# Differenced value rows in stick-breaking attention, and later table loads in the state-space scan

## What is computed

```python
def stick_breaking_attention(q, k, v):      # A[t,s] = beta_ts * prod_{s<j<t}(1 - beta_tj), s < t
...
        log_beta = jax.nn.log_sigmoid(z)
        log_1m = jnp.where(causal, log_beta - z, 0.0)
        later = lax.cumsum(log_1m, axis=3, reverse=True) - log_1m
        w = jnp.where(causal, jnp.exp(log_beta + later), 0.0)
        outs.append(jnp.einsum('bhqk,bkhd->bqhd', w.astype(v.dtype), v[:, :kv_len]))
```

```python
def s5_mixer(xn, w_in, ...):                # grouped state-space model, chunkwise scan, then a gated projection
    u = (xn @ w_in).astype(f32)
...
        bu = jnp.einsum('tbgh,gph->tbgp', u_t.astype(jnp.complex64), b_bar)
        a_cum, s = lax.associative_scan(binop, (a_elems, bu), axis=0)
        y = jnp.einsum('tbgp,ghp->tbgh', s, c_mat).real
```

## Time and profile before

| what | us |
|---|---|
| median of 3 runs (2297.76 to 2300.46) | 2300.3 |
| the profiled execution, whole | 2300.35 |
| its span, first to last instruction | 2298.6 |
| PE busy | 2239.3 (97%) |
| DVE busy | 1275.2 (55%) |
| ACT busy | 984.8 (43%) |
| POOL busy | 394.9 (17%) |

### The profile page before, as it was taken

One profiled execution on the slowest core, in us unless ns is written; L12 is line 12 of the kernel. 1 busy time (PEld: TensorE's weight loads), 2 busy tenths in 40 slices (PEclk: granted clock), 3 DMA queues, 4 the chain that ended last, 5 costly groups with the idle time before them and its releaser, 6 DMA issues.

```text
span 2298.6 us, 30269 instructions
## 1 busy us (share of the span) xinstructions
PE 2239.3 (97%) x11479; PEld 1806.8 (79%) x11479; DVE 1275.2 (55%) x2273; ACT 984.8 (43%) x1835; POOL 394.9 (17%) x472
## 2 busy tenths in 40 slices
PE   7899999999999999999979999999999999999999
PEld 6777777688877787878868888888888668888887
DVE  6965565755645444454583555464444685554643
ACT  7445555533554545363432423233344654232322
POOL 7742131126202030300000000000034230000000
PEclk9999999999999999999999999999999999999999
DMA  7354212134232222315462232322222102323222
GB/s 224 117 170 128 74 56 92 43 105 161 97 119 62 87 89 77 97 60 192 147 212 86 80 110 80 104 92 93 91 99 88 52 19 74 110 87 97 92 102 81
DMA packets 182444, 232.51 MB, mean 101 GB/s; under 512 B 29499, under 2 KB 110866, under 8 KB 182302
## 3 DMA queue, kind: packets, MB, share of 16 engines
q1 hardware_dynamic: 159406, 205.64, 27.9%
q10 hardware_dynamic: 22896, 24.94, 3.4%
HBM read 213.74 MB, written 21.00 MB: 102 GB/s over the span
## 4 chain that ended last, share of the span: by engine, by line
PE 87%; DVE 6%; issue 2%; ACT 2%; POOL 1%; DMA 1%; SPq 0%; ACTq 0%; POOLq 0%; DVEq 0%
PE G L2199 25%; PE G L2201 25%; PE G L2200 25%; DVE w_lo L1756 1%; PE X L2208 1%; PE X L2319 1%; PE X L2330 1%; PE X L2307 1%; PE X L2333 1%; DMA big<-s_u 1%; PE X L2303 1%; POOL big L1235 1%; PE X L2218 1%; DVE u_lo L1801 1%; PE X L2311 1%
## 5 line engine op out<-in xcount | busy, mean ns | idle before, releaser
L2199 PE MATMUL G<-w_hi,u_hi 128*128 128x512 f32 x1536 | 622.1, 405 | 4.0 <-issue 2.1
L2201 PE MATMUL G<-w_hi,u_lo 128*128 128x512 f32 x1536 | 600.9, 391 | 0.0
L2200 PE MATMUL G<-w_lo,u_hi 128*128 128x512 f32 x1536 | 599.2, 390 | 0.0
L1756 DVE SCALAR_TENSOR_TENSOR w_lo<-raw,par,w_hi 128x512 fp32r<-128x512 f32 x496 | 373.3, 791 | 401.1 <-ACT w_hi L1256 398.1
L1256 ACT ACTIVATE w_hi<-raw,par 128x512 fp32r<-128x512 f32 x496 | 318.2, 714 | 342.1 <-PE G L2201 340.2
L2199 PE MATMUL G<-u_hi,w_hi 128*128 128x512 f32 (+1 forms) x1168 | 458.3, 392 | 0.3 <-DVE w_lo L1756 0.2
L2201 PE MATMUL G<-u_hi,w_lo 128*128 128x512 f32 (+1 forms) x1168 | 446.0, 382 | 0.0
L2200 PE MATMUL G<-u_lo,w_hi 128*128 128x512 f32 (+1 forms) x1168 | 446.0, 382 | 0.0
L2199 PEld LDWEIGHTS G<-w_hi,u_hi 128*128 128x128 f32 x1536 | 289.1, 188 | 71.0 <-issue 9.3
L2201 PEld LDWEIGHTS G<-w_hi,u_lo 128*128 128x128 f32 x1536 | 288.5, 188 | 62.2
L2200 PEld LDWEIGHTS G<-w_lo,u_hi 128*128 128x128 f32 x1536 | 289.3, 188 | 59.4 <-issue 1.9
(11 more groups left out here) (316 smaller groups left out, 2388.8 us busy)
## 6 DMA issues: line engine op xcount, KB each, us to landing
raw<-in_ffn_w_up SPq DMA_DIRECT2D x88, 512.0 KB, 4.7
raw<-in_e_w_in SPq DMA_DIRECT2D x56, 512.0 KB, 4.7
raw<-in_o_w_in SPq DMA_DIRECT2D x56, 512.0 KB, 4.5
raw<-in_ffn_w_down SPq DMA_DIRECT2D x40, 512.0 KB, 4.3
raw<-in_e_w_out SPq DMA_DIRECT2D x16, 512.0 KB, 4.6
raw<-in_o_w_out SPq DMA_DIRECT2D x16, 512.0 KB, 4.3
raw<-in_a_w_glu SPq DMA_DIRECT2D x16, 512.0 KB, 4.5
raw<-in_w_kv SPq DMA_DIRECT2D x16, 512.0 KB, 4.6
```

What stands on the lines that cost most here:

```text
L1756: V.scalar_tensor_tensor(w_lo[:, n % HL, k], raw[:, n % RAW, k], gain(name, k0 + k), w_hi[:, n % HL, k].bitcast(F32), ALU.mult, ALU.subtract)\
L2199: pe.matmul(out, lh, rh, start=start, stop=False)
L2200: pe.matmul(out, lh, rl, start=False, stop=False)
L2201: return pe.matmul(out, ll, rh, start=False, stop=stop)
```

## The change

Stick-breaking: the differences of the products are no longer made, neither on DVE nor on POOL, and the buffers and memsets for them go. PE transposes the products themselves, as soon as two rounds after the scores (three before), and sums three rounds after them (four before), so the stage has one slot less, and three of its rounds instead of four are hosted by the value chunk. ACT's copy out of the transpose becomes 1 - x, an Identity with scale -1 and a bias read from a column of ones. The scan that reuses a buffer now waits for the transpose of its old content, where it waited for the differencing. The values are differenced instead, once: behind the last block of each value chunk ACT issues a copy of its rows, shifted down by one partition, into rows 16 to 19 of big (127 partitions, and one more DMA for the rows that cross a tile), and DVE subtracts it from the values, 128 by 512 at a time, four times for each chunk: for the first chunk in the host's positions 3 to 6, for the second in rounds 8 to 11.

State-space: ACT issues zl(4) and zl(5) in slot 8 and zl(6) and zl(7) in slot 9, all behind a new wait for the load of u(7).

The diff, its core:

```diff
@@ -481,39 +481,37 @@
+            s.values = (values - 1, values)
-            s.slots = s.rounds + 5
+            s.slots = s.rounds + 4
-            plan_chunks([("v", "N", dict(dst=1, step=2))], [(s, -4)])
-            stage("between", host=s, host_at=4, host_end=s.slots)
+            plan_chunks([("v", "N", dict(dst=1, step=2))], [(s, -5)])
+            for a in range(2):
+                for m in range(4):
+                    mark("value_step", s.i, a, m)
+            stage("between", host=s, host_at=3, host_end=s.slots)
...
@@ -678,6 +676,7 @@
+        S5_NEXT = {8: (4, 5), 9: (6, 7)}
@@ -853,10 +852,11 @@
-        def sb_weight(t):
-            i = t // 2 % TT
-            o = 8192 + P * (i * (i + 1) + t % 2 * (i + 1))
-            return bigf[:, o:o + P * (i + 1)]
+        value_shifted = sem("value_shifted")
+        row_before = big[:, 16:20, :]
+
+        def value_rows(a):
+            return att[:, 0:8, :].rearrange("p (t a) n -> p t a n", a=2)[:, :, a, :]
@@ -1219,21 +1219,6 @@
-                if n == sb_down.n:
-                    for t, (hd, i) in enumerate(sb_mix.steps):
...
-                        pool.wait_ge(*at_("sb_product", sb_mix.i, t))
-                        if t >= 2 * TT:
-                            pool.wait_ge(*at_("sb_turned", sb_mix.i, t - 2 * TT))
-                        pool.tensor_tensor(sb_weight(t)[:, 0:L - 1], sb_prod(t)[:, 1:L], sb_prod(t)[:, 0:L - 1],
-                                           ALU.subtract).then_inc(*by(sb_step(t), sb_mix.i, t))
@@ -1387,12 +1372,20 @@
+            def shift_values(chunk, a):
+
+                act.wait_ge(*at_("operand", chunk, "v", 3))
+                if a:
+                    act.wait_ge(*at_("value_step", sb_mix.i, 0, 3))
+                act.dma_start(row_before[1:P, :, :], value_rows(a)[0:P - 1, :, :]).then_inc(value_shifted, 16)
+                act.dma_start(row_before[0:1, 1:4, :], value_rows(a)[P - 1:P, 0:3, :]).then_inc(value_shifted, 16)
@@ -1402,13 +1395,14 @@
-                if 0 <= u - 3 < s.rounds:
-                    n = P * ((u - 3) % TT + 1)
-                    for t in (2 * u - 6, 2 * u - 5):
+                if 0 <= u - 2 < s.rounds:
+                    n = P * ((u - 2) % TT + 1)
+                    for t in (2 * u - 4, 2 * u - 3):
                         if t >= 4:
-                            act.wait_ge(*at_("sb_summed", s.i, u - 5))
+                            act.wait_ge(*at_("sb_summed", s.i, u - 4))
                         act.wait_ge(*at_("sb_turned", s.i, t))
-                        nc.scalar.activation(sb_turned(t)[:, 0:n], G[:, t % SB_TURN, 0:n], ACT.Copy)\
+                        nc.scalar.activation(sb_turned(t)[:, 0:n], G[:, t % SB_TURN, 0:n], ACT.Identity,
+                                             bias=one_c, scale=-1.0)\
                             .then_inc(*by("pt_copied", s.i, t))
@@ -1528,8 +1522,10 @@
-                    if k < 4:
-                        s5_load_zl(k + 4)
+                if t == 8:
+                    act.wait_ge(s5_u_loaded[KT - 1], 16)
+                for k in S5_NEXT.get(t, ()):
+                    s5_load_zl(k)
@@ -1630,6 +1626,8 @@
                                         .then_inc(*by("operand", s.i, "v", m))
+                                    if m == 3 and s.i in sb_mix.values:
+                                        shift_values(s.i, s.dst)
@@ -1974,6 +1972,14 @@
+            def value_step(a, m):
+
+                dve.wait_ge(value_shifted, 32 * (a + 1))
+                if a == 0 and m == 0:
+                    link("dve", dve, V.memset(row_before[0:1, 0, :], 0.0))
+                v = value_rows(a)[:, m, :]
+                V.tensor_tensor(v, v, row_before[:, m, :], ALU.subtract).then_inc(*by("value_step", sb_mix.i, a, m))
@@ -1987,16 +1993,12 @@
                     if t >= 4:
-                        dve.wait_ge(*at_(sb_step(t), s.i, t - 4))
+                        dve.wait_ge(*at_("sb_turned", s.i, t - 4))
                     V.tensor_tensor_scan(sb_prod(t)[:, 0:L][:, ::-1], sb_keep(t)[:, 0:L][:, ::-1],
                                          bias_tile[:, 384 - P * i:512][:, ::-1], 1.0, ALU.mult, ALU.max)\
                         .then_inc(*by("sb_product", s.i, t))
-                t = 2 * u
-                dve.wait_ge(*at_("sb_product", s.i, t))
-                if t >= 2 * TT:
-                    dve.wait_ge(*at_("sb_turned", s.i, t - 2 * TT))
-                V.tensor_tensor(sb_weight(t)[:, 0:L - 1], sb_prod(t)[:, 1:L], sb_prod(t)[:, 0:L - 1],
-                                ALU.subtract).then_inc(*by(sb_step(t), s.i, t))
+                if 2 * TT <= u < 3 * TT:
+                    value_step(1, u - 2 * TT)
@@ -2048,6 +2050,8 @@
+                        if s.host is sb_mix and 3 <= b < 7:
+                            value_step(0, b - 3)
@@ -2345,28 +2349,28 @@
-                if 0 <= u - 3 < s.rounds:
-                    if u == 3:
-                        pe.wait_ge(*at_("sb_zero", s.i))
-                    for t in (2 * u - 6, 2 * u - 5):
-                        pe.wait_ge(*at_(sb_step(t), s.i, t))
+                if 0 <= u - 2 < s.rounds:
+                    for t in (2 * u - 4, 2 * u - 3):
+                        pe.wait_ge(*at_("sb_product", s.i, t))
                         pe.wait_ge(*(at_("pt_copied", s.i, t - SB_TURN) if t >= SB_TURN else at_(*s.gfreed[t])))
-                        for j in range((u - 3) % TT + 1):
-                            ins = pe.transpose(G[:, t % SB_TURN, j * P:(j + 1) * P], sb_weight(t)[:, j * P:(j + 1) * P],
+                        for j in range((u - 2) % TT + 1):
+                            ins = pe.transpose(G[:, t % SB_TURN, j * P:(j + 1) * P], sb_prod(t)[:, j * P:(j + 1) * P],
                                                ident[:, :])
                         ins.then_inc(*by("sb_turned", s.i, t))
-                if 0 <= u - 4 < s.rounds:
-                    pair, i = (u - 4) // TT, (u - 4) % TT
+                if 0 <= u - 3 < s.rounds:
+                    pair, i = (u - 3) // TT, (u - 3) % TT
...
                     if i == 0:
                         pe.wait_ge(*(at_("sb_y", s.i, pair - 1) if pair else at_(*s.gfreed[SB_SUM])))
+                        if pair % TT == 0:
+                            pe.wait_ge(*at_("value_step", s.i, pair // TT, 3))
```

More of the change, by code:

```diff
@@ L483, in plan_sb @@
             values = len(plan)
+            s.values = (values - 1, values)
             s.steps = [(2 * p + e, i) for p in range(s.heads // 2) for i in range(TT) for e in range(2)]
             s.rounds = len(s.steps) // 2
-            s.slots = s.rounds + 5
+            s.slots = s.rounds + 4
             s.gfreed = [("operand", values, "v", m) for m in range(4)]
-            plan_chunks([("v", "N", dict(dst=1, step=2))], [(s, -4)])
-            stage("between", host=s, host_at=4, host_end=s.slots)
-            for u in range(4, s.slots):
+            plan_chunks([("v", "N", dict(dst=1, step=2))], [(s, -5)])
[3 more added lines that the diff above has]
+            stage("between", host=s, host_at=3, host_end=s.slots)
+            for u in range(3, s.slots):
                 plan_sb_slot(s, u)
@@ L507, in plan_sb_slot @@
                     mark("sb_product", s.i, t)
-                    mark(sb_step(t), s.i, t)
-            if 0 <= u - 3 < s.rounds:
-                for t in (2 * u - 6, 2 * u - 5):
+            if 0 <= u - 2 < s.rounds:
+                for t in (2 * u - 4, 2 * u - 3):
                     mark("sb_turned", s.i, t)
                     mark("pt_copied", s.i, t)
-            if 0 <= u - 4 < s.rounds:
-                mark("sb_summed", s.i, u - 4)
-            if u - 5 >= 0 and (u - 5) % TT == TT - 1:
-                mark("sb_y", s.i, (u - 5) // TT)
+            if 0 <= u - 3 < s.rounds:
+                mark("sb_summed", s.i, u - 3)
+            if u - 4 >= 0 and (u - 4) % TT == TT - 1:
+                mark("sb_y", s.i, (u - 4) // TT)
         def plan_down(kt, first=0, host=None, host_at=0, y=None):
@@ L1388, in act_slot @@
                     act.wait_ge(*at_("aux_ready", s.aux["ot" if s.akind == "A" else "pv", s.heads - 1]))
+            def shift_values(chunk, a):
[4 more added lines that the diff above has]
+                act.dma_start(row_before[0:1, 1:4, :], value_rows(a)[P - 1:P, 0:3, :]).then_inc(value_shifted, 16)
             def act_sb(s, u):
-                if u - 5 >= 0 and (u - 5) % TT == TT - 1:
-                    act.wait_ge(*at_("sb_summed", s.i, u - 5))
-                    nc.scalar.activation(big[:, (u - 5) // TT, :], G[:, SB_SUM, :], ACT.Copy)\
-                        .then_inc(*by("sb_y", s.i, (u - 5) // TT))
+                if u - 4 >= 0 and (u - 4) % TT == TT - 1:
+                    act.wait_ge(*at_("sb_summed", s.i, u - 4))
+                    nc.scalar.activation(big[:, (u - 4) // TT, :], G[:, SB_SUM, :], ACT.Copy)\
+                        .then_inc(*by("sb_y", s.i, (u - 4) // TT))
                 if u < s.rounds:
@@ L2347, in pe_sb @@
```

(14 more changed lines are left out.)

18 lines of the change are left out of this document (1 added, 17 removed).

## The result

| | before | after |
|---|---|---|
| median of the runs, us | 2299.3 (2297.8 to 2300.5, 4 runs) | 2354.0 (2353.5 to 2355.6, 4 runs) |
| ratio after / before | | 1.0235, 95% interval 1.0221 to 1.0248 |
| span of the profiled execution, us | 2298.6 | 2352.4 |
| busy PE, us | 2239 | 2242 |

A forecast was written before the change was run, and what follows sets the result against it. PE carries 87% of the chain, so savings count only where PE waits or runs at the lower clock. 5.3 + 2.7 + 1.5 + 1.7 - 1.25 = 9.95 us off 2300.35 gives 2290.4 us, range 2287.0 to 2295.5.

The forecast's parts named there:

- the start of the stick-breaking stage: Behind the value chunk, PE's 0.69 us wait for ACT becomes about 1.95: +1.25 us, between +0.5 and +2.5.
- The cover that I named: First chunk's row copy, 7 to 9 us, is covered: DVE has nothing to do before the high part preceding ACT's table load.
- issue two copies: At the stick-breaking start, ACT's two copy issues cost 0.33 us and up each, 0.8 in all.
- has until round 8: Stick-breaking: the second chunk's row copy is not needed until round 8.
- State-space, -5.3: u(4) lands earlier, PE's 4.66 us wait before V(4) goes, DVE's chains and B(4) shift: -5.3 us, -5.4 to -3.5.
- Rival 2: State-space: ACT's new wait for u(7) delays zl(4) and Y(4), taking the 5.3 us gain; 2295.7 us, chance 0.08.
- Steady part, -2.7: Stick-breaking rounds: differences go, PE sets the pace, late rounds four apart 8.54 us instead of 9.38: -2.7 us.
- rival 3: Stick-breaking: the shorter distance makes PE wait in every 512 round, so the gain does not come; 2295 us, chance 0.06.
- The end, -1.5 and -1.7: Stick-breaking end: PE's 1.65 us wait shrinks to about 0.15 (-1.5), low clock before the last sums goes (-1.7).
- one fewer: Clock case: the second low-clock stretch, after the stick-breaking stage, may not come; 2288.7 us, chance 0.11.
- rival 1: Clock: new PE waits may bring 1.2 GHz stretches, 2292.1 or 2293.8 us (0.13), or one fewer comes, 2288.7 (0.11).
- Rival 4: Stick-breaking: Identity outside Sigmoid's table gives every round two table loads on ACT, 70 us longer; 2360 us, chance 0.04.

The follow-up runs named there:

- e6_cut_126: The whole change with the copy of 127 rows cut into 126 + 1; 2292.9 us against 2300.1 for the kernel before.
- e1_split: The whole change with the copy of 127 rows cut into 112 + 15; 2292.6 us against 2299.0 for the kernel before, ratio 0.9974.
- e5_sp_issue: The whole change with rows copied in 112 + 15 and the copies issued on SP's queue, not ACT's; 2286.3 us against 2300.1 for the kernel before.
- e4_swapped: The changed kernel with its two copies issued in the other order, the little one first, the 127 rows last; 2352.5 us.
- e2_tables: The kernel before with the state-space part of the change alone, stick-breaking as before; 2292.2 us, ratio 0.9971.
- e9_values_sp: Kernel before plus the stick-breaking part alone, rows in 112 + 15, copies issued on SP's queue; 2291.7 us against 2299.7, ratio 0.9965.

## Why the prediction was wrong

**The failed step.** It is the start of the stick-breaking stage, priced at +1.25 us and at most +2.5; it came to 62.3 us more of waiting and some 3.7 of low clock. The term in it that failed is the copy of the rows: "half as much takes 6.9 us in the full stretch, so 7 to 9 us". I took bytes from a load of 128 rows and gave the copy the same width. It moved its megabyte in 43 us. The cover that I named, up to ACT's table load about 12 us later, was right in kind and 30 us short. The prediction asked nowhere how many engines share the copy. With the height 127 held against the rule that the other heights bear out (e6_cut_126), and by 26 GB/s an engine, which these traces show, the sum would have come out on the side of slower.

**The second failed step**, of the same edit: "issue two copies (0.33 and up each, 0.8 in all)". My bound came from one short issue. Behind a copy on one engine an issue was held 33.5 and 34.1 us. And even at full width, three issues took 3.9 us (e1_split). I had named what stands behind ACT at the start (high part, sigmoids, the copy that PE waits for) and that each would be late by as much; only the amount was wrong. With it, PE's wait at the start is 36.1 us in the kernel after, 4.97 in e1_split and 1.00 in e5_sp_issue, against a forecast of 1.95 and at most 3.2 (0.69 + 2.5). The terms of that forecast, 0.8 for the issues and 0.65 for the sigmoids, also sum to 1.45 and not to its 1.25; with no issue on ACT, e5_sp_issue shows 0.31 over the 0.69 of before. The second copy "has until round 8": enough for data that lands in 6 us, but in e4_swapped DVE waits 26.9 us for it, and in the kernel after it was its issue that PE paid for.

**State-space, -5.3: right.** u(4) lands 6.9 us after its issue instead of 13.4, and the 4.66 us wait is gone. PE's timeline, before (a row ahead of the stretch, for the offset that the execution already had) and after:

```profile
1166.67 1.12 PE L2441 MATMUL X<-att,big 128*64 128x128 f32 x16 [0.95 <-DVE work L1964]
```

```profile
1165.44 1.11 PE L2445 MATMUL X<-att,big 128*64 128x128 f32 x16 [0.94 <-DVE work L1962]
...
1186.84 1.17 PE L2419 MATMUL X<-big,att 128*64 128x64 f32 x32 [2.68 <-DVE work L1962]
1189.87 1.15 PE L2445 MATMUL X<-att,big 128*64 128x128 f32 x16 [0.78 <-DMA att<-s_toeplitz]
1193.61 1.15 PE L2428 MATMUL X<-ident,work 64*64 64x64 f32 x32 [1.56 <-DVE work L1962]
```

B(4) starts at 1193.61 against 1200.35, 6.74 earlier, of which 1.23 were there at the first row: 5.5 us, for 5.35 forecast. V(7) now waits for DVE (2.68), no longer for a load, as the step has it. The new wait's price is visible and small: Y(4) waits 0.78 us for its table, and B(4) still waits for DVE, so nothing of it reaches the end. Rival 2 is false. Over whole runs the part is worth 6.8 us (e2_tables, 4.6 to 8.7).

**Steady part, -2.7: right.** In the kernel after, behind the two copies, PE's first matmuls of rounds four apart (before: the earlier trace rows), and DVE's scans:

```profile
1906.78 0.49 PE L2350 MATMUL X<-big,att 64*128 64x128 f32 x4
...
1915.31 0.49 PE L2350 MATMUL X<-big,att 64*128 64x128 f32 x4
...
1923.85 0.49 PE L2350 MATMUL X<-big,att 64*128 64x128 f32 x4
```

```profile
1921.06 1.81 DVE L1997 TENSOR_TENSOR_SCAN work<-att,bias_tile 128x384 f32<-128x384 f32 x2 [1.26 <-ACT att L1396]
1923.62 1.23 DVE L1997 TENSOR_TENSOR_SCAN work<-att,bias_tile 128x512 f32<-128x512 f32 x1 [0.76 <-ACT att L1396]
```

8.54 us to the last, where it was 9.38; DVE waits for ACT in each round. The 1 - x copies take 534 ns in the median (L1404) against 446 for the plain ones (L1411), 0.09 more each, within the 0 to 0.1 of the forecast. The shorter distance between scores and transpose costs nothing in the steady part: rival 3 is false.

**The end, -1.5 and -1.7: right.** The wait of 1.65 us is 0.19 + 0.17, and no low clock comes before the last sums. The 2.13 us wait stayed. The stretch at half clock behind it stayed in the kernel after (0.66 over 1939 to 1943) and did not come in e5_sp_issue, which has the form of the case "one fewer" of rival 1. Its reason, that the wait before the last sums is gone, does not hold: that wait is gone in the kernel after and in e9_values_sp as well, and there the stretch comes (granted clock 0.79 over 1881 to 1889 in e9_values_sp, 1.00 over 1871 to 1879 in e5_sp_issue, with the same stage of 95.1 us). What decides it stays open, and it is luck of the execution as far as these runs show. Without the start, the stick-breaking terms sum to -5.9; the stage of e5_sp_issue measured -5.9 with a start wait that is 0.3 longer than before.

**Rival 4** (table loads for Identity) is false: there are as many table loads as before, and in e5_sp_issue the stage's table load stands once ahead of its first sigmoid.

So the forecast for the kernel with its copies at full width and off ACT would have been 2290.4 + (1.0 - 1.95) = 2289.5, and 2287.8 for an execution without the second stretch (1.7), for 2286.3 measured. The rest of the gap is of the size of what the state-space part gave over its forecast (6.8 for 5.3). Every other step was read from rows of the same work; the copy was priced by bytes, and the issues by one issue in a quiet place.

## What to carry to other kernels

Price a DMA by its shape and not by its bytes: ask first how many engines its outer dimension lets it use, and treat a height such as 127 as a warning, because cutting it into 126 + 1 or 112 + 15 cost one more issue here and was worth 61 us. A DMA issue is an instruction of the engine that carries it: at 1.2 us each, and tens of us behind a narrow copy, it belongs on a queue that nobody waits for. And when a transfer is said to be hidden, multiply it by ten and see what stands behind it in the queue of its issuer and of its reader; here the reader's queue alone cost 60 us (e4_swapped against e1_split), and in the kernel after it was the issuer's that both waits ended on.

## What the runs showed of the hardware

- A copy of 127 rows of four 2 KB runs, within the on-chip memory: 26 GB/s, 43 us. 126 rows: some 260 GB/s. 112 + 15: 270 GB/s. 124 rows: 57 to 102 GB/s.
- An issue on ACT's queue behind a copy that lies on one engine is held until about a hundred of its packets are left (99 to 105): 33.5 and 34.1 us behind 508 packets, 3.5 and then about 10 us each behind copies of 127. Behind 124 rows on four engines it is held 4.8 us.
- A burst of three issues on ACT took 3.2 to 3.9 us (e1_split, e6_cut_126), where a single one elsewhere takes 0.33; SP's took 3.6 (e5_sp_issue), and PE's waits show nothing of it.
- PE ran at 1.2 GHz for a while behind every wait of 4.45 us or more (such as 36, 27, 7.38, 4.97, 4.80 and 4.45 us) and did not behind one of 1.00 us in the same place; before, it did behind one of 1.65 us and not behind one of 2.95.
